# A two-layer encoder kernel: TensorE's work is issued by finer due times, head turns one transposition at a time, and a layer's first weight tiles are split in another order

## The chip, the cores and the metric

One core of a Trainium2 chip. The metric is the device time of the kernel in microseconds. Engines: PE is TensorE's matmul, PEld its weight load, DVE is VectorE, ACT is ScalarE, SP starts the DMA transfers of the weights, POOL is nearly unused.

## The reference, cut to what matters

```python
DEPTH = 2; SEQ = 512; D_MODEL = 1024
def hybrid_layer(x, ...):
    h = rms_norm(x, norm1_g)
    (a_q, a_k, a_v, b_q, b_k, b_v, c_qkv, d_cq, d_ckv, d_kr, gates) = split(h @ w_in)
    oa = windowed_gqa(a_q, a_k, a_v, ...)            # A: 8 heads, window 128
    ob = differential_attention(b_q, b_k, b_v, ...)  # B: 4 heads x 2 maps, all keys, then rms_norm
    oc = dilated_attention(c_qkv, ...)               # C: three patterns C0, C1, C2
    od = latent_attention(d_cq, d_ckv, d_kr, ...)    # D: q and k from low ranks, 8 heads
    merged = sum(sigmoid(gates_i) * (o_i @ w_branch[i]) for the four)
    x = x + merged @ w_o
    u = depthwise_conv(rms_norm(x, norm2_g) @ ffn_w_up)
    g, up = split(u)
    return x + (silu(g) * up) @ ffn_w_down
```

## The kernel before

Both layers are one loop body. Each engine has its own program, written by several streams (Python generators) that are merged: a stream yields a due time, and `together` always lets the stream with the smallest due time emit its next piece. The due times are in steps of TensorE's dense work; `ORDER` gives each block of dense matmuls its START and END. The merged order is fixed when the program is built; on the chip the engines meet through semaphores only.

Dense work (`dense`, `block`): a block is one projection of 512 columns for the 512 tokens, in four PSUM banks (PJ). A weight tile of two 128-row chunks is used by all four banks, one bank a step. The weights arrive in float32; ScalarE rounds a tile to a high half `wh` (L776), VectorE takes the rest as `wl` (L1139), and each product is three float32r matmuls, high by high, high by low, low by high (`split3`, L452 to L454). With two chunks that is six matmuls a step, 24 for a tile, 96 for a block of 16 steps. Tiles are held in three slots, raw tiles in two; SP sends for raw tile k when tile k-2 has been split (`tile_split`). In the blocks of C1 and C2 the tokens are taken in the order of their residues modulo 4, so TensorE's stationary operand is read with a stride of four elements (`perm` in `tokens_out`).

Turns (`turns`, `turn`): once a block of queries or keys is evacuated and normed by VectorE, each 128-token tile is turned by up to four transpositions (L503) into the bank TD, from where ScalarE and VectorE each copy half. `turn` waits for the norm (`normed`) and for TD's last copies, then issues its transpositions. There are 69 turns in a layer. The due times of a block's four turns are 2 steps apart (1.25 or 1.5 for some).

Attention (`attention`): a unit is one head of one query tile. TensorE makes its scores S (L655) into S1, VectorE adds the bias and takes the minimum, ScalarE takes the exponential (L1019), TensorE transposes the probabilities T (L503) into TA, ScalarE copies one half (L1027) and VectorE, behind it, the other (L1563), TensorE multiplies by the values V (L665) into O1. `WINDOW` gives each pattern a stretch of steps, which `slots` divides evenly: with the pace p of a unit, S is due at the start, V of the unit two earlier a third of p later, T of the unit one earlier two thirds later. C0 runs beside the blocks of C1, C1 and C2 beside those of C2, kv and cq, D mostly in a pause without dense work, A beside Bq, Bk and Bv, B beside gate3a to br3b (gates and branch projection of D's output).

The dense stream yields once a step, so S, V, T and turns are only placed between whole steps. A float32 matmul shows two records, a transposition one.

After pattern B, `turns` of VectorE norms oB, and four turns bring it to gTh/gTl for br1a. ScalarE issues the parameter transfers for the next layer behind the last gate of gate3a (L874).

A layer begins with the squares of x on ScalarE (L833), the norm's scale on VectorE (L1208 to L1214), the splits of the first three weight tiles, the copy of the turned parameters (`params_in`, L1063, L1065, L1646), and then eight chunks of transpositions of the normed x (L539), each copied by ScalarE (L841) and VectorE (L1221). The transpositions wait for the parameters' copy, since TD is one of their banks.

## Time and profile before

| | us |
|---|---|
| median of 3 runs | 3001.43 (2998.47 to 3010.02) |
| the profiled execution | 3004.72 |
| its span | 3002.9 |
| TensorE busy in it | 2820.7 (94%), 13358 matmuls |
| TensorE weight loads | 2267.0 (75%) |
| VectorE busy | 1566.0 (52%) |
| ScalarE busy | 1179.0 (39%) |
| DMA moved | 217.62 MB, mean 72 GB/s |

The busy time of TensorE is from the start of a matmul to its modelled end, and neighbours overlap: a dense matmul is listed with 0.39 us, while the next starts 0.23 us later. Distances between starts are what can be added up. A row of a timeline with x4 holds four like instructions in a row. Stretches of the table by windows are the blocks of the first layer, found by counting dense matmuls (96 to a block): 112.9 to 246.6 is C1q, C1k, C1v; 655.7 to 700.4 is Bq; 846.2 to 884.2 is br3a; 957.8 begins gate0a; 1152 to 1495 is most of the feed-forward part.

### The profile page before, as it was taken

What the parts mean: (1) busy time and instruction counts of PE and PEld (TensorE: products, weight loads), DVE (VectorE), ACT (ScalarE), POOL (GpSimd) and SP (SyncE); (2) the same over time, 40 slices, a digit from 0 to 9 for tenths busy, and PEclk for the clock granted to TensorE, in tenths of its full rate; (3) what the DMA queues carried; (4) which work ended last, traced back from release to release, by engine and by line L of the source; (5) the groups of instructions that cost most, each with busy time, mean ns of one, the idle gap of its engine ahead of it and who ended that gap; (6) DMA issues with size and microseconds to landing.
All of it is one profiled execution on the core that took longest, in us unless ns stands there. A gap on an engine that the chain in (4) does not pass through costs nothing.

```text
span 3002.9 us, 44753 instructions
## 1 busy us (share of the span) xinstructions
PE 2820.7 (94%) x13358; PEld 2267.0 (75%) x13358; DVE 1566.0 (52%) x3238; ACT 1179.0 (39%) x2387; POOL 0.6 (0%) x5
## 2 busy tenths in 40 slices
PE   5999989989989998999979999898899899999998
PEld 4889978666667887888868898776666678788887
DVE  5454476444445445555644544764354454465655
ACT  4444444434433234332434444534444332342432
POOL 0000000000000000000000000000000000000000
PEclk9999999889999999999989999999999999999999
DMA  4212222001112332333332122220111123223332
GB/s 152 72 48 72 78 63 85 12 29 41 45 37 78 94 96 78 99 98 99 99 100 64 44 78 79 67 85 1 36 43 50 31 91 98 92 85 98 95 96 91
DMA packets 141819, 217.62 MB, mean 72 GB/s; under 512 B 14777, under 2 KB 69387, under 8 KB 141195
## 3 DMA queue, kind: packets, MB, share of 16 engines
q1 hardware_dynamic: 132521, 200.62, 21.4%
q10 hardware_dynamic: 9058, 14.06, 1.4%
q8 instruction: 118, 1.93, 0.3%
q14 instruction: 122, 1.00, 0.1%
HBM read 206.20 MB, written 8.45 MB: 71 GB/s over the span
## 4 chain that ended last, share of the span: by engine, by line
PE 81%; DVE 9%; ACT 4%; issue 4%; ACTq 1%; DMA 1%; DVEq 0%; SPq 0%
PE bank L452 21%; PE bank L454 20%; PE bank L453 20%; PE bank L665 7%; PE bank L655 6%; PE bank L503 5%; DVE s_work L1563 1%; DVE s_wl L1139 1%; ACT s_wh L776 1%; ACT s_work L1027 1%; DVE s_work L1294 1%; PE bank L539 1%; ACTq L874 1%; DMA s_raw<-in_w_in 0%; ACT s_work L1019 0%
## 5 line engine op out<-in xcount | busy, mean ns | idle before, releaser
L1139 DVE TENSOR_TENSOR s_wl<-s_raw,s_wh 128x1024 fp32r<-128x1024 f32 (+2 forms) x372 | 453.6, 1220 | 526.5 <-ACT s_wh L776 525.9
L776 ACT ACTIVATE s_wh<-s_raw 128x1024 fp32r<-128x1024 f32 (+2 forms) x372 | 392.2, 1055 | 625.1 <-PE bank L454 591.9
L452 PE MATMUL bank<-s_hTh,s_wh 128*128 128x512 f32 x1216 | 486.2, 400 | 4.5 <-DVE s_work L1231 4.5
L454 PE MATMUL bank<-s_hTh,s_wl 128*128 128x512 f32 x1216 | 476.9, 392 | 0.0
L453 PE MATMUL bank<-s_hTl,s_wh 128*128 128x512 f32 x1216 | 476.7, 392 | 0.0
L452 PE MATMUL bank<-s_wh,s_hTh 128*128 128x512 f32 (+1 forms) x1088 | 475.8, 437 | 0.0
L454 PE MATMUL bank<-s_wh,s_hTl 128*128 128x512 f32 (+1 forms) x1088 | 427.0, 392 | 0.0
L453 PE MATMUL bank<-s_wl,s_hTh 128*128 128x512 f32 (+1 forms) x1088 | 426.7, 392 | 0.0
L1019 ACT ACTIVATE s_work<-s_work,s_stat 128x128 f32<-128x128 f32 (+3 forms) x384 | 214.1, 558 | 369.5 <-DVE s_stat L1588 123.0
L1563 DVE COPY s_work<-bank 128x256 f32<-128x256 f32 (+1 forms) x288 | 105.2, 365 | 394.5 <-ACT s_work L1027 391.9
L503 PE MATMUL bank<-s_consts,s_work 128*128 128x128 f32 (+1 forms) x1560 | 250.0, 281 | 47.3 <-DVE s_gTl L1495 14.3
L452 PEld LDWEIGHTS bank<-s_wh,s_hTh 128*128 128x128 f32 x1088 | 252.5, 232 | 47.9 <-issue 24.3
L452 PEld LDWEIGHTS bank<-s_hTh,s_wh 128*128 128x128 f32 x1216 | 230.1, 189 | 67.2 <-issue 16.7
L454 PEld LDWEIGHTS bank<-s_wh,s_hTl 128*128 128x128 f32 x1088 | 252.6, 232 | 27.2
L453 PEld LDWEIGHTS bank<-s_wl,s_hTh 128*128 128x128 f32 x1088 | 256.5, 236 | 20.9 <-issue 0.5
L655 PE MATMUL bank<-s_work 64*128 64x384 f32 (+4 forms) x640 | 267.6, 511 | 1.4 <-DVE s_work L1584 0.9
L454 PEld LDWEIGHTS bank<-s_hTh,s_wl 128*128 128x128 f32 x1216 | 230.1, 189 | 49.3
L453 PEld LDWEIGHTS bank<-s_hTl,s_wh 128*128 128x128 f32 x1216 | 230.3, 189 | 44.5
L503 PEld LDWEIGHTS bank<-s_consts,s_work 128*128 128x128 f32 (+1 forms) x1560 | 193.3, 148 | 89.1 <-DVE s_gTl L1495 17.0
L665 PEld LDWEIGHTS bank<-s_work 128*128 128x128 f32 x1280 | 167.4, 193 | 100.8 <-DVE s_work L1563 48.8
L665 PE MATMUL bank<-s_work 128*128 128x64 f32 (+1 forms) x1280 | 183.1, 280 | 31.4 <-DVE s_work L1563 30.6
L1027 ACT ACTIVATE s_work<-bank 128x256 f32<-128x256 f32 (+1 forms) x288 | 102.8, 357 | 201.0 <-PE bank L503 181.0
(166 smaller groups left out, 3199.6 us busy)
## 6 DMA issues: line engine op xcount, KB each, us to landing
s_raw<-in_w_in SPq DMA_DIRECT2D x168, 512.0 KB, 3.4
s_raw<-in_ffn_w_up SPq DMA_DIRECT2D x176, 256.0 KB, 2.9
s_raw<-in_ffn_w_down SPq DMA_DIRECT2D x44, 512.0 KB, 3.7
s_raw<-in_w_branch SPq DMA_DIRECT2D x32, 512.0 KB, 3.6
s_raw<-in_w_o SPq DMA_DIRECT2D x16, 512.0 KB, 3.6
x_keep<-s_work ACTq DMA_DIRECT2D x2, 2048.0 KB, 7.5
s_raw<-in_w_in SPq DMA_DIRECT2D x16, 256.0 KB, 2.9
s_work<-x_keep ACTq DMA_DIRECT2D x2, 2048.0 KB, 8.2
```

The source lines that it names most:

```text
L452: mm(out, stationary[0], moving[0], start=start, stop=False)
L453: mm(out, stationary[0], moving[1], start=False, stop=False)
L454: return mm(out, stationary[1], moving[0], start=False, stop=stop)
L503: last = nc.tensor.transpose(dst[0:m, n * P:n * P + k], src, ident[0:k, 0:k])
L539: last = nc.tensor.transpose(dst[:, t * P:t * P + P], h_sb[:, t, P * c:P * c + P], ident)
L655: last = mm(out, st, mv, start=True, stop=True)
L665: last = mm(out, st, mv, start=start, stop=stop)
L776: a(wh[:, k % 3, 0:n], raw[:, s, 0:n], ACT.Copy).then_inc(*hi_split.up(own))
L1019: a(probs[:, u % 2, x0:x0 + w], scores[:, u % 2, x0:x0 + w], ACT.Exp, scale=-1.0, bias=stat[:, mins, c:c + 1], accum_out=stat[:, sums, c:c ...
L1027: a(probsT[:, u % 2, P * lo:P * mid], src[:, P * lo:P * mid], ACT.Copy).then_inc(*ta_act.up(own))
L1139: v.tensor_tensor(wl[:, k % 3, 0:n], raw[:, k % 2, 0:n], wh[:, k % 3, 0:n].bitcast(F32), ALU.subtract).then_inc(*tile_split.up(own))
L1563: v.tensor_copy(probsT[:, u % 2, P * mid:P * hi], src[:, P * mid:P * hi]).then_inc(*ta_dve.up(own))
```

## The change

Four things, of which the first three move TensorE's instructions and none changes what is computed. (1) `block` yields before every dense matmul, at sixths of a step, so all other pieces are placed between single matmuls. (2) A turn's transpositions are yielded a sixth of a step apart, so that dense matmuls stand between them; its semaphore is raised by the last. Transpositions of attention keep together (pace 0). (3) Pattern B's window ends at START["gate1a"] - 4 instead of START["gate0a"], 91 steps long instead of 47; `B_NORM` is that end, and the norm of oB, its turns (B_NORM + 9 on) and their copies follow it, as does the transfer that brings x back. (4) At the start of a layer, ScalarE splits tiles 0 and 1 before the squares and tile 2 behind the second chunk of the norm; VectorE splits tile 0 before the norm, tile 1 behind the copy of the parameters, tile 2 behind the second chunk.

```diff
@@ -141,8 +141,9 @@
     END[name] = START[name] + steps
 WINDOW = dict(
     C0=(START["C1q"] + 1, START["C2q"], 32), C1=(START["C2q"] + 1, START["kv"], 8), C2=(START["kv"] + 1, START["gate2a"], 8),
-    D=(START["Aq"] + 14, START["Bq"], 32), A=(START["Bq"], START["gate3a"], 32), B=(START["gate3a"] + 1, START["gate0a"], 32),
+    D=(START["Aq"] + 14, START["Bq"], 32), A=(START["Bq"], START["gate3a"], 32), B=(START["gate3a"] + 1, START["gate1a"] - 4, 32),
 )
+B_NORM = WINDOW["B"][1]
 def build(nc, io):
@@ -447,11 +448,9 @@
             holder = [(pj_dve, b - 3) for b in range(4)]
-            def split3(out, stationary, moving, start, stop):
-
-                mm(out, stationary[0], moving[0], start=start, stop=False)
-                mm(out, stationary[0], moving[1], start=False, stop=False)
-                return mm(out, stationary[1], moving[0], start=False, stop=stop)
+            def split3(stationary, moving):
+
+                return (stationary[0], moving[0]), (stationary[0], moving[1]), (stationary[1], moving[0])
             def block(name, ntiles, operands, by, chunks=2, cols=512, width=512, first=lambda i, b: None):
@@ -468,9 +467,13 @@
                             taken[by] += 1
                             holder[b] = (by, taken[by])
                         first(i, b)
+                        n = 0
                         for c in range(chunks):
-                            st, mv = operands(b, chunks * i + c, [t[:, c, :] for t in w])
-                            last = split3(PJ[b][:, 0:width], st, mv, i == 0 and c == 0, i == ntiles - 1 and c == chunks - 1)
+                            for st, mv in split3(*operands(b, chunks * i + c, [t[:, c, :] for t in w])):
+                                if n:
+                                    yield START[name] + 4 * i + b + n / (3 * chunks)
+                                n += 1
+                                last = mm(PJ[b][:, 0:width], st, mv, start=i == 0 and n == 1, stop=i == ntiles - 1 and n == 3 * chunks)
                         if i == ntiles - 1:
                             last.then_inc(*pj_ready.up())
                         elif b == 3:
@@ -496,12 +499,14 @@
             H, G = (hTh, hTl), (gTh, gTl)
-            def transposed(dst, sources, at=0):
-
-                for n, src in enumerate(sources, at):
+            def transposed(dst, sources, done, when, pace, at=0):
+
+                for n, src in enumerate(sources):
+                    if n:
+                        yield when + n * pace
                     k, m = src.shape[0], src.shape[1]
-                    last = nc.tensor.transpose(dst[0:m, n * P:n * P + k], src, ident[0:k, 0:k])
-                return last
+                    last = nc.tensor.transpose(dst[0:m, (at + n) * P:(at + n) * P + k], src, ident[0:k, 0:k])
+                last.then_inc(*done.up())
             def turned(n):
@@ -585,14 +590,15 @@
                             *hidden_lo.at(l, hidden + 2 * i + 2)) if half == "a" and b == 0 else None)
                     hidden += 2 * size
-            def turn(sources, *ready):
-
+            def turn(when, sources, *ready):
+
+                yield when
                 for handle, count in ready:
                     pe.wait_ge(handle, count)
                 pe.wait_ge(*td_act.at(l, n_turn[0]))
                 pe.wait_ge(*td_dve.at(l, n_turn[0]))
-                transposed(TD, sources).then_inc(*td_ready.up())
                 n_turn[0] += 1
+                yield from transposed(TD, sources, td_ready, when, 1 / 6)
             def turns():
@@ -601,9 +607,8 @@
                 def head_turns(begin, sources_of, pace=2.0):
                     nonlocal n
                     for t in range(4):
-                        yield begin + pace * t
                         n += 1
-                        turn(sources_of(t), normed.at(l, n))
+                        yield from turn(begin + pace * t, sources_of(t), normed.at(l, n))
                 def chunks_of(src):
                     return lambda t: [src[:, t, P * c:P * c + P] for c in range(4)]
...
@@ -627,8 +631,7 @@
                 yield from head_turns(END["Bq"] + 6, chunks_of(stage))
                 yield from head_turns(END["Bk"] + 6, chunks_of(stage))
                 for t in range(4):
-                    yield START["gate0a"] + 10 + 1.25 * t
-                    turn([oB[:, t, P * c:P * c + P] for c in range(4)], sublayer_normed.at(l, t + 1))
+                    yield from turn(B_NORM + 9 + 1.25 * t, [oB[:, t, P * c:P * c + P] for c in range(4)], sublayer_normed.at(l, t + 1))
             def attention(name, scores_of, values_of, per_out, begun, keys=all_keys, tile_of=None):
@@ -644,7 +647,7 @@
                         pe.wait_ge(*ta_act.at(l, n_att[0]))
                         pe.wait_ge(*ta_dve.at(l, n_att[0]))
                         n_att[0] += 1
-                        transposed(TA, tile_of(tile)).then_inc(*ta_ready.up())
+                        yield from transposed(TA, tile_of(tile), ta_ready, at, 0)
                     if step < n:
                         yield at
                         if step == 0:
@@ -673,7 +676,7 @@
                         pe.wait_ge(*ta_dve.at(l, n_att[0]))
                         n_att[0] += 1
                         group[u] = n_att[0]
-                        transposed(TA, [probs[:, u % 2, P * k:P * k + P] for k in range(lo, hi)], at=lo).then_inc(*ta_ready.up())
+                        yield from transposed(TA, [probs[:, u % 2, P * k:P * k + P] for k in range(lo, hi)], ta_ready, at + 2 * pace / 3, 0, at=lo)
             def token_values(v_of, width, places, keys=all_keys):
                 def values_of(u, out, pt):
...
@@ -832,9 +835,11 @@
                         act.wait_ge(*own.done(l))
                         a(h_sb[:, t, cols], x_sb[:, t, cols], ACT.Square, accum_out=stat[:, 0, 4 * half + t:4 * half + t + 1]).then_inc(*ssum.up(own))
-            def norm_out(row):
+            def norm_out(row, after_two=lambda: None):
                 for c in range(DC):
+                    if c == 2:
+                        after_two()
                     n_norm[0] += 1
                     act.wait_ge(*nt_ready.at(l, n_norm[0]))
                     act.wait_ge(*own.done(l))
...
@@ -1055,15 +1060,15 @@
                 act.wait_ge(*x_moved.at(l, 1))
                 act.dma_start(x_sb, keep).then_inc(*x_moved.up())
+            split_next()
+            split_next()
             squares(-8)
-            for _k in range(3):
-                split_next()
             src = group()
             act.wait_ge(*own.done(l))
             a(prm[:, 0:NROW], src[:, 0:NROW], ACT.Copy).then_inc(*act_step.up(own))
             act.wait_ge(*own.done(l))
             a(prm[:, NROW:NROW + 88], src[:, P:P + 88], ACT.Copy).then_inc(*td_act.up(own))
-            norm_out(ROW["norm1"])
+            norm_out(ROW["norm1"], split_next)
             act.dma_start(keep, x_sb).then_inc(*x_moved.up())
             for n, name in enumerate(("d_q_norm", "d_k_norm")):
                 direct(rope_rows[:, n, :], io[name][L, NOPE:DQK].broadcast_to([P, ROPE]))
...
@@ -1509,7 +1516,7 @@
                 yield from q_out(END["Aq"] + 6, qA, 0)
                 yield from q_out(END["Bq"] + 6, qT, 4)
                 yield from k_out(END["Bk"] + 6, kT, "bk")
-                begin = START["gate0a"] + 1
+                begin = B_NORM
                 for t in range(4):
                     yield begin + 2 + 0.9 * t
                     dve.wait_ge(*own.done(l))
@@ -1636,20 +1643,20 @@
                                      keys=near_keys, tile_at=4)
                 yield from attention("B", biased_b, out_b, 4)
+            split_next()
             normalise()
-            for _k in range(3):
-                split_next()
             dve.wait_ge(*params_in.at(l, 0))
             src = group()
             dve.wait_ge(*own.done(l))
             v.tensor_copy(prm[:, NROW + 88:NROW + 176], src[:, 256:344]).then_inc(*td_dve.up(own))
+            split_next()
             for at, n, key in ((0, 4, "aq"), (4, 4, "bq"), (8, 12, "cqn")):
                 dve.wait_ge(*own.done(l))
                 v.tensor_scalar(gain[:, at:at + n], consts[:, 128 + at:128 + at + n], prm[:, ROW[key]:ROW[key] + 1], None, ALU.mult).then_inc(*dve_step.up(own))
             dve.wait_ge(*own.done(l))
             v.tensor_scalar(gain[:, 21:22], prm[:, ROW["dq"]:ROW["dq"] + 1], -DQK ** -0.5, None, ALU.mult).then_inc(*gains_in.up(own))
-            norm_out(ROW["norm1"])
+            norm_out(ROW["norm1"], split_next)
             together(dense(), turns(), attentions(), splits())
     for name, s in signals.items():
```

## Rows read from the trace of the kernel before

**Rows 1.** The page: the span, and the chain that ended last, by engine.

```profile
span 3002.9 us, 44753 instructions
...
PE 81%; DVE 9%; ACT 4%; issue 4%; ACTq 1%; DMA 1%; DVEq 0%; SPq 0%
```

**Rows 2.** Busy time by stretches: length, each engine's busy us, granted clock, DMA share, GB/s.

```profile
112.90:246.60 133.70, 132.49 (x626) 109.91 (x626) 60.26 (x164) 56.21 (x140) 0.00 (x0) 1.00 0.16 49
...
655.70:700.40 44.70, 42.29 (x194) 29.38 (x193) 17.34 (x46) 18.86 (x55) 0.00 (x0) 0.97 0.20 60
...
846.20:884.20 38.00, 30.54 (x135) 21.02 (x133) 13.24 (x31) 9.70 (x21) 0.00 (x0) 0.87 0.10 31
...
1152.00:1495.00 343.00, 343.00 (x1516) 284.08 (x1517) 203.75 (x240) 128.46 (x154) 0.00 (x0) 1.00 0.31 96
```

**Rows 3.** Timeline of TensorE in C0v: start us, listed us, engine, line, operation.

```profile
98.73 0.60 PE L503 MATMUL bank<-s_consts,s_work 128*128 128x128 f32 x4
...
99.40 0.40 PE L453 MATMUL bank<-s_wl,s_hTh 128*128 128x512 f32 x1
```

**Rows 4.** The same in C2k, where tokens are read with a stride.

```profile
303.11 0.39 PE L454 MATMUL bank<-s_wh,s_hTl 128*128 128x512 f32 x1
303.34 0.60 PE L503 MATMUL bank<-s_consts,s_work 128*128 128x128 f32 x4
...
304.13 0.40 PE L453 MATMUL bank<-s_wl,s_hTh 128*128 128x512 f32 x1
```

**Rows 5.** The same in C1q, strided too: scores (L655) and values (L665).

```profile
145.40 0.91 PE L655 MATMUL bank<-s_work 64*128 64x384 f32 x2
...
146.70 0.40 PE L453 MATMUL bank<-s_wl,s_hTh 128*128 128x512 f32 x1
...
150.22 0.91 PE L655 MATMUL bank<-s_work 64*128 64x384 f32 x2
151.06 0.88 PE L665 MATMUL bank<-s_work 128*128 128x64 f32 x6
151.78 0.50 PE L503 MATMUL bank<-s_consts,s_work 128*128 128x128 f32 x3
...
154.58 0.88 PE L665 MATMUL bank<-s_work 128*128 128x64 f32 x6
...
155.71 0.40 PE L453 MATMUL bank<-s_wl,s_hTh 128*128 128x512 f32 x1
```

**Rows 6.** The same in gate3a, where nothing is strided.

```profile
821.53 1.12 PE L655 MATMUL bank<-s_work 64*128 64x512 f32 x2
...
822.92 0.39 PE L453 MATMUL bank<-s_hTl,s_wh 128*128 128x512 f32 x1
...
826.90 1.12 PE L655 MATMUL bank<-s_work 64*128 64x512 f32 x2
827.95 1.16 PE L665 MATMUL bank<-s_work 128*128 128x128 f32 x8
```

**Rows 7.** Timeline at the start of the second layer, VectorE and TensorE.

```profile
1515.09 0.16 DVE L1208 TENSOR_TENSOR s_stat<-s_stat 128x4 f32<-128x4 f32 x1 [2.64 <-issue]
...
1520.54 2.35 DVE L1139 TENSOR_TENSOR s_wl<-s_raw,s_wh 128x1024 fp32r<-128x1024 f32 x2
...
1528.13 0.25 DVE L1646 COPY s_prm<-bank 128x88 f32<-128x88 f32 x1
...
1534.29 0.47 PE L452 MATMUL bank<-s_wh,s_hTh 128*128 128x512 f32 x1
```

**Rows 8.** Timeline of TensorE in br3a; in brackets the idle time before.

```profile
858.42 2.08 PE L665 MATMUL bank<-s_work 128*128 128x128 f32 x8 [7.46 <-DVE s_work L1563]
```

**Rows 9.** Timeline of VectorE and TensorE at the start of gate0a.

```profile
956.89 0.68 DVE L1231 SCALAR_TENSOR_TENSOR s_work<-s_work,bank 128x512 f32<-128x512 f32 x1
...
973.05 1.42 DVE L1524 TENSOR_TENSOR s_work<-s_work,s_stat 128x512 f32<-128x512 f32 x2
...
973.96 0.65 PE L503 MATMUL bank<-s_consts,s_work 128*128 128x128 f32 x4 [1.05 <-DVE s_work L1524]
```

More of the change, by code:

```diff
@@ L616, in turns @@
                 for t in range(4):
-                    yield END["cq"] + 14 + 1.5 * t
-                    turn([oC[:, 0, t, P * c:P * c + P] for c in range(4)], combined.at(l, t + 1))
+                    yield from turn(END["cq"] + 14 + 1.5 * t, [oC[:, 0, t, P * c:P * c + P] for c in range(4)], combined.at(l, t + 1))
                 for hb in range(2):
                     for t in range(4):
-                        yield END["dq1"] + 13.2 + 5 * hb + 1.25 * t
-                        turn([(stage, stage_b)[hb][:, t, DQK * h:DQK * h + DQK] for h in range(4)], normed.at(l, n + 1))
+                        yield from turn(END["dq1"] + 13.2 + 5 * hb + 1.25 * t,
+                                        [(stage, stage_b)[hb][:, t, DQK * h:DQK * h + DQK] for h in range(4)], normed.at(l, n + 1))
                 n += 1
@@ L730, in _ @@
             pe.wait_ge(*params_in.at(l, 0))
-            turn([rows[:, n, :] for n in range(3)])
+            together(turn(0, [rows[:, n, :] for n in range(3)]))
             together(dense(), turns(), attentions())
@@ L989, in turns @@
                 for t in range(4):
-                    yield START["gate0a"] + 10.4 + 1.25 * t
+                    yield B_NORM + 9.4 + 1.25 * t
                     hi_out(gTh[:, 0:4, P * t:P * t + P], group(), td_act, gain[:, 20:21])
@@ L1214, in normalise, with norm_out @@
                     v.tensor_scalar(h_sb[:, t, :], x_sb[:, t, :], stat[:, 2, t:t + 1], None, ALU.mult).then_inc(*h_normed.up(own))
-            def norm_out(row):
+            def norm_out(row, after_two=lambda: None):
                 for c in range(DC):
+                    if c == 2:
+                        after_two()
                     n_norm[0] += 1
```

## The prediction

> **What bounds the kernel now.** I read the page first: the profiled execution took 3004.72 us around a span of 3002.9 us, and 81% of the chain that ended last lies on TensorE's matmuls [rows 1]. Then a table by stretches. In the feed-forward part (1152 to 1495) TensorE is busy all the time, 1516 matmuls in 343.00 us, 0.226 us each; the change touches nothing there. In the stretch of the second dilated pattern's projections (112.9 to 246.6) it is busy 132.49 of 133.70 us, so whatever is added to its queue lengthens the kernel. From 655.7 it idles a few per cent, and from 846.2 to 884.2 it idles 7.5 us at a granted clock of 0.87 [rows 2]. So for most of what the diff touches the question is what TensorE's own queue costs in its new order, and only in a few places which wait goes. Then the timeline, for the price of one neighbour beside another, since a matmul's listed duration overlaps the next and only distances between starts add up.
>
> **The order.** TensorE's order follows from the due times alone (`together` takes the smallest), so it can be written out for both kernels. A step is one bank's six dense matmuls, 6 x 0.227 = 1.36 us. Before, everything else lands only between whole steps, and parts due within one step form one run ("V6 T3"). After, each dense matmul has a due time of its own, so scores S, values V and transpositions T, due a third of a unit apart, land apart. Counting in both orders how often a run ends and a dense matmul follows (an "exit"), per layer: T 112 before, 342 after; V 56 and 112; S 58 and 114. Of these, in the six blocks C1q to C2v, whose stationary operand is read with a stride of four ("strided"): T 28 and 92, V 23 and 40, S 23 and 40. The numbers of matmuls stay the same.
>
> **Price of an exit.** Plain: four T start at 98.73 and the second dense matmul behind them at 99.40. Taking off one dense distance, 0.227, and three T-to-T distances of 0.109 (the start listed for the first dense one is modelled early, so I go by the second), the last T to the first dense one takes 0.116 [rows 3]. That is 0.007 more than T to T: a plain exit is nearly free. Strided: 303.34 to 304.13, less 0.235 (the distance of dense neighbours there, 0.23 at 303.11) and 0.327, leaves 0.228 [rows 4]: 0.119 more than T to T, because the strided weights are loaded behind only a short transposition. V: six V and then T take 151.06 to 151.78, 0.72; six V and then the dense one take 154.58 to 155.71 less 0.235, 0.895: an exit costs 0.175. S: two S and then V take 0.84, two S and then the dense one 146.70 - 145.40 - 0.235 = 1.065: 0.225 [rows 5]. Plain S: 822.92 - 821.53 - 0.227 = 1.16 against 827.95 - 826.90 = 1.05: 0.11 [rows 6]. Plain V lies at 0.175 less the 0.112 by which strided and plain differ for T: 0.06; I take that for the 64-column V of pattern A and nothing for the 128-column ones. Going from a dense matmul into T or V costs nothing beyond the dense distance (0.23 at 303.11) [rows 4], and into S as much as before.
>
> The sum per layer: strided 64 x 0.119 + 17 x 0.175 + 17 x 0.225 = 7.6 + 3.0 + 3.8 = 14.4 us. Plain: T 166 x 0.007 = 1.2, V 22 x 0.06 = 1.3, S 39 x 0.11 = 4.3, together 6.8. So 21 us a layer, 42 in both. Of it the split of the turns themselves is small: 69 turns x 3 new exits, 48 of them strided (the four turns each of C1q, C1k, C2q and C2k, which fall beside strided blocks): 48 x 0.119 + 159 x 0.007 = 6.8 us a layer, 14 in both; the rest is the finer grid. The row that is missing is a T alone between two dense matmuls. From below: if the next dense weights were fetched together with the T's under one long matmul, the exit would cost nothing and the T less than its 0.109; from above: nothing suggests over 0.228 for strided ones. I take the measured exits, since the loads in every row run one ahead.
>
> The Trainium skill ("TensorE: Matmul & The Clock Gate", LDWEIGHTS) says that a load takes its number of columns over 1.2 GHz, 107 ns, whatever else. The plain rows agree (0.109 and 0.116), the strided ones do not (0.228); by the rule the strided exits would cost as the plain ones and the sum would be some 14 us smaller for T alone. The same page (Step-by-step) lets the engine pull loads ahead of matmuls in flight through a deep window; what that would make of this change is the second rival.
>
> **Start of a layer.** Before, in the second layer: the sum of squares is ready and VectorE starts at 1515.09, normalises until 1520.6, splits tiles 0 and 1, waits for tile 2 (whose transfer waits for tile 0's split), splits it, and only then copies the parameters at 1528.13, for which the norm's transpositions wait; the first dense matmul starts at 1534.29, 6.2 us later [rows 7]. After: VectorE splits tile 0 first (1.22 us), normalises (5.5), and copies at about 1522.0. ScalarE's two splits now stand before its squares, which costs it nothing before the last squares' data arrive except some 1 us of queue, hidden by VectorE's first split. Behind the copy VectorE has one split (1.22) more before the norm's low halves and one more after two chunks; the last transpositions wait for VectorE's chunks, so from copy to the first dense matmul I count 7 instead of 6.2. First dense at about 1529: 5 us earlier. In layer 0 the two splits of ScalarE delay the squares by 2.8 instead; gain 3. Together -8 (0 if the copy is no longer last, -13 if nothing is added behind it). Moving tile 0's split forward also lets SP's transfer of tile 2 start some 5 us sooner, off the path.
>
> **Pattern B's window** runs over 91 instead of 47 steps. Its work is the same, with more cover: before, 5 of 32 units have no dense matmul between a unit's T and V; after, at least 10. But its two large waits stay. In br3a TensorE waits 7.46 us [rows 8] while ScalarE issues 15 parameter DMAs in a row, behind which the copy of a transposed tile is queued; at half the density TensorE has some 3 us more of other work: -3 (0 to -10, with the low clock behind it). At the end, oB is normed on VectorE beside the branch's own evacuation: before, that took from 956.89 to 973.05 and the first turn waited 1.05 us [rows 9]. That turn was due 10 steps behind the block that it follows; now it is due 5 behind br0b. Same work (16 us), 5 steps (6.8 us) less cover, dense tile splits between: the first oB turn waits about 6, and with its transpositions spread over half a step the three next ones about 1 each, +5 against before (0 to +9). Small waits -2. Net 0 a layer (-12 to +9).
>
> **Pattern A's window**: T to V is 6 dense matmuls before in all 32 units and 5 after; the waits there (some 10 us a layer) stay. A third or so of the plain 6.8 us falls where TensorE waits anyway: -1.5 a layer. Turns on VectorE's heels (cq, oC) are paced by VectorE and keep their time. Splitting any turn delays its completion by three dense matmuls, 0.7 us; at a pace of 2 steps (2.7 us) that is covered.
>
> **Sum.** +42 - 3 - 8 + 0 = +31 us on the profiled execution. The median shown (3001.43) lies 3.3 below that execution; the difference is applied to the median: 3032 us.
>
> **Rivals.**
> (1) The forecast: exits as priced, waits about as before. 3015 to 3050, likeliest 3032. Chance 0.65.
> (2) Faster: the loads hide. If one 512-column matmul covers both the T's load and that of the dense one behind it, exits cost nothing, and each spread T costs about half its present 0.109, so a turn (0.44 us now) saves 0.22. Decides from the point at which two loads fit ahead. 138 turns x 0.22 = 30, plus 8 from the start: 2963; if only the exits are free, 2993. Against it: in the rows a dense load behind a T is never cheaper than T to T. Chance 0.12, at about 2978.
> (3) No difference: the finer places take the waits for ScalarE's and VectorE's copies out of patterns A and B. Up to 20 us a layer are there (7.46 of it the DMA burst); all gone, 42 - 40 - 8 = -6: 2995. Against it: T to V grows only in B, and the two large waits have other causes. Chance 0.15, at about 3003.
> (4) Slower still: the copies come too late in C0 as well, since T to V is 5 dense matmuls instead of 6 in 26 of its 32 units; 0.3 us x 32 x 2 = +19, and the waits at oB drop the clock: 3055. Chance 0.08.
> That the change does only what its title says is no case: the diff puts every part on the finer grid. If it did (turns alone), the sum would be 14 - 8 = +6.
>
> About 0.5%, 15 us, can be told from no change. Slower by more (over 3016): 0.73; within: 0.16; faster: 0.11. The range from 2993 to 3054 leaves out most of (2) and the tail of (4).
>
> **What would show it.** Exits: C1q to C1v longer by about 11 us a layer (133.7 to 145) at full clock with no new idle time, C2q to C2v by 3; T alone between dense matmuls at 0.23 behind the one before, and 0.34 (plain) or 0.46 (strided) from T to the second dense one. Start: the copy of the parameters within 7.5 us of the sum of squares and the first dense matmul 5 us sooner. B: a wait of 4 to 5 us in br3a and one of about 6 before the oB turns in gate1a. It would be wrong if spread T in strided blocks showed T to dense well below 0.2, or if pattern A lost its waits.

## The result, and the profile after

The changed kernel takes 3025.99 us (median; 3021.69 to 3030.5), 1.0073 of the time before (95% interval 1.0054 to 1.0092): slower, by 24.6 us at the medians, each of five executions. The profiled execution of after took 3021.69 us around a span of 3019.9, that of before 3004.72: 17.0 us between the two that are compared below. The page of after, against [rows 1]: the same number of instructions, a longer span, and one point more of the chain on TensorE.

```profile
span 3019.9 us, 44753 instructions
...
PE 82%; DVE 8%; issue 4%; ACT 3%; ACTq 1%; DMA 0%; DVEq 0%; SPq 0%
```

The table by stretches, with the columns of [rows 2]: the dilated pattern's strided blocks C1q to C1v, Bq, br3a, gate1a, the feed-forward part.

```profile
110.50:252.60 142.10, 142.01 (x626) 114.39 (x626) 60.59 (x164) 56.68 (x140) 0.00 (x0) 1.00 0.15 47
664.60:708.90 44.30, 44.02 (x195) 29.92 (x194) 17.39 (x46) 19.32 (x56) 0.00 (x0) 0.93 0.20 60
837.00:863.70 26.70, 22.63 (x94) 15.60 (x93) 9.59 (x18) 6.08 (x12) 0.00 (x0) 0.87 0.15 44
1023.70:1057.10 33.40, 26.46 (x114) 19.76 (x113) 20.39 (x36) 8.68 (x11) 0.00 (x0) 0.95 0.21 64
1157.00:1500.00 343.00, 342.94 (x1516) 284.06 (x1515) 203.98 (x241) 128.59 (x155) 0.00 (x0) 1.00 0.31 96
```

C1q to C1v were 133.7 us and are 142.1, with the same 626 matmuls, TensorE busy throughout and the clock at full: the loss is in the queue's own order. The feed-forward part is unchanged. br3a has lost 11 of its 38 us, since its window ends later, and still idles 4 us. gate1a idles 6.9, where it had no idle time before (21.8 us long then).

Cut by the first dense matmul of each block, with starts from the timeline, both layers together (the 8.3 us behind the last dense matmul are in neither column):

| us | before | after | difference |
|---|---|---|---|
| to the first dense matmul | 43.2 | 39.5 | -3.7 |
| C0q to C0v | 139.5 | 141.9 | +2.4 |
| C1q to C2v (strided) | 458.8 | 482.0 | +23.2 |
| kv to gate2b, dk (turns of cq, dq) | 356.8 | 366.0 | +9.2 |
| Aq and the pause behind it | 262.5 | 260.3 | -2.2 |
| Bq to Bv (pattern A) | 281.7 | 273.9 | -7.8 |
| gates and branches (pattern B) | 597.0 | 598.0 | +1.0 |
| o0, o1 | 114.3 | 114.1 | -0.2 |
| feed-forward, without its last block | 685.7 | 685.7 | 0 |
| down2b, start of layer 1 in it | 55.2 | 50.2 | -5.0 |

The row of Aq hides two things. From the first to the last of Aq's own 96 dense matmuls a layer it is +5.2 us (52.7 to 57.9, all at full clock), and the pause behind them is -7.4 (209.8 to 202.4), with 28.9 us at the low clock instead of 41.7.

### The profile page after: what moved, and what is told of

The parts are those of the page before. It is cut to its first block, busy times and chain, and to the rows that moved or that the text cites. A ratio compares the mean times of both kernels' runs of the same rounds, so it can differ in the third digit from the quotient of the medians.

```text
span 3019.9 us, 44753 instructions
## 1 busy us (share of the span) xinstructions
PE 2855.5 (95%) x13358; PEld 2258.9 (75%) x13358; DVE 1567.3 (52%) x3238; ACT 1179.7 (39%) x2387; POOL 0.6 (0%) x5
## 4 chain that ended last, share of the span: by engine, by line
PE 82%; DVE 8%; issue 4%; ACT 3%; ACTq 1%; DMA 0%; DVEq 0%; SPq 0%
PE bank L476 63%; PE bank L668 7%; PE bank L658 7%; PE bank L508 6%; DVE s_wl L1144 1%; DVE s_work L1570 1%; ACT s_work L1032 1%; ACT s_wh L779 1%; DVE s_work L1301 1%; ACTq L879 1%; PE bank L544 0%; DMA s_raw<-in_w_in 0%; DVE s_work L1304 0%; DVE s_gTl L1471 0%; ACT s_work L1024 0%
## 5 line engine op out<-in xcount | busy, mean ns | idle before, releaser
L476 PE MATMUL bank<-s_hTl,s_wh 128*128 128x512 f32 x1216 | 487.9, 401 | 0.0
L476 PE MATMUL bank<-s_hTh,s_wl 128*128 128x512 f32 x1216 | 487.1, 401 | 0.0
L476 PE MATMUL bank<-s_wl,s_hTh 128*128 128x512 f32 (+1 forms) x1088 | 474.6, 436 | 0.0
L476 PE MATMUL bank<-s_wh,s_hTh 128*128 128x512 f32 (+1 forms) x1088 | 461.2, 424 | 0.0
L476 PE MATMUL bank<-s_wh,s_hTl 128*128 128x512 f32 (+1 forms) x1088 | 460.3, 423 | 0.0
L508 PE MATMUL bank<-s_consts,s_work 128*128 128x128 f32 (+1 forms) x1560 | 311.0, 280 | 55.4 <-DVE s_gTl L1502 13.4
L508 PEld LDWEIGHTS bank<-s_consts,s_work 128*128 128x128 f32 (+1 forms) x1560 | 203.2, 143 | 112.2 <-issue 19.5
L476 PEld LDWEIGHTS bank<-s_wh,s_hTh 128*128 128x128 f32 x1088 | 254.5, 234 | 43.6 <-issue 18.9
L668 PEld LDWEIGHTS bank<-s_work 128*128 128x128 f32 x1280 | 174.0, 193 | 33.0 <-DVE s_work L1570 15.2
L668 PE MATMUL bank<-s_work 128*128 128x64 f32 (+1 forms) x1280 | 172.0, 272 | 13.4 <-DVE s_work L1570 13.0
```

What stands on the lines that cost most here:

```text
L476: last = mm(PJ[b][:, 0:width], st, mv, start=i == 0 and n == 1, stop=i == ntiles - 1 and n == 3 * chunks)
L508: last = nc.tensor.transpose(dst[0:m, (at + n) * P:(at + n) * P + k], src, ident[0:k, 0:k])
L668: last = mm(out, st, mv, start=start, stop=stop)
```

## Experiments

"By trace" is the difference of such cuts against the kernel before, or against the kernel named, both layers together. The number behind a median is its ratio to the kernel before on the same chip, with its 95% interval. Of each edit the main lines are shown.

### One part at a time

**e1_start**: the kernel before with the new order at a layer's start.

```
-            squares(-8)
-            for _k in range(3):
-                split_next()
+            split_next()
+            split_next()
+            squares(-8)
```

> The kernel before with part (4) of the change alone: tiles 0 and 1 split by ScalarE before the squares, tile 0 by VectorE before the norm, tile 1 behind the parameters' copy, tile 2 behind the second chunk. Theory: the first dense matmul of a layer comes 3.6 us sooner in layer 0 and 5.1 in layer 1 (as in the changed kernel's trace), nothing else moves: -8 to -9 us, about 2993. Rival: part of it is given back at the next wait: under -4.

Measured 2996.22 us, 0.9972 (0.9955 to 0.9988). By trace the first dense matmul comes 4.1 us sooner in layer 0, and the last block with layer 1's start is 5.1 shorter: 9.2, as forecast.

**e4_bwin**: the kernel before with pattern B's longer window alone.

```
-B=(START["gate3a"] + 1, START["gate0a"], 32)
+B=(START["gate3a"] + 1, START["gate1a"] - 4, 32)
```

> The kernel before with pattern B's window of 91 steps alone, on whole steps, turns together, old start. Theory: the wait at the DMA burst shrinks from 7.5 to about 4 us and its low clock with it, a wait of 5 to 6 us before the oB turns comes in gate1a: -2 to -5 us a layer, about 2994. Rival (B's stalls are in its own units and go with the cover): -10 a layer, about 2981; or the oB wait eats all: same.

Measured 2999.32 us, 0.9982 (0.9969 to 0.9994): a gain of some 5 us by the ratio, by trace 4.3 in gates and branches. br3a idles 4.0 instead of 7.5 a layer, gate1a 4.9 and 5.3 instead of 0. The window trades one wait for another and keeps a little.

**e2_grid**: the change without split turns, without the new start and window: dense matmuls and attention on the fine grid.

```
-                yield from transposed(TD, sources, td_ready, when, 1 / 6)
+                yield from transposed(TD, sources, td_ready, when, 0)
```

> Due times at sixths of a step for the dense work, but each turn's transpositions together, pattern B's old window and the old start. Theory of exits: C1q to C2v +10 us a layer (26 T, 17 V and 17 S exits in strided blocks), in plain blocks +6 of exits, of which pattern A gives back more by shorter waits: +14 to +22 in all, about 3018. Rival (the finer grid is for free, the turns cost): within 4 us of before.

Measured 3007.35 us, 1.0009 (0.9996 to 1.0022): far less than expected. By trace +2.3, of very unequal parts: strided blocks +13.0, C0 +2.2, kv to dk +1.1, gates -1.8, pattern A -6.9 (idle 17.8 to 8.3), and -6.2 in Aq and its pause, nearly all of it the clock (below). The strided exits are there. Pattern A's waits are mostly gone, against the prediction; the expectation of this run had allowed for that, but not for so little from the plain exits.

**e3_turns**: the opposite half: split turns, attention back on whole steps, old start and window.

```
-                        yield at
+                        yield math.floor(at) + 0.99
```

> A turn's transpositions one at a time between dense matmuls, all of attention kept between whole steps, old window, old start: what the title says. Theory of exits: 48 exits in strided blocks at 0.12 us are +5.7 us a layer in C1k, C1v, C2k, C2v, and up to 3 a layer of waits for later turns in C0k, dq0 and gate2b: +11 to +18 in all, about 3015. Rival (loads hide behind the dense matmul): -10 or faster.

Measured 3045.15 us, 1.0135 (1.0116 to 1.0155), twice the upper end expected. By trace +36.9: strided blocks 13.9, kv to dk 9.1, gates 5.1, C0 2.4, pattern A 1.6, Aq 2.6. Two of these are no exits at all: 9.1 where the turns follow VectorE closely, and the 5.1.

**e9_together**: the changed kernel with a turn's transpositions together again, all else kept (the edit of e2_grid on it).

> The changed kernel with each turn's transpositions together again (pace 0), all else as changed. Theory after e1 to e4: start -8, grid +3 and window -5 leave -10 against the kernel before, so the turns' split alone is worth 30 us or more of the changed kernel: about 2996 (before 3006). Of it 10 in the strided blocks, 8 in the stretch kv to br2b, 4 in the gates. Rival (the split's cost in e3 came from its attention on whole steps): 3012 to 3018.

Measured 3010.1 us, 1.0021 (1.0004 to 1.0037), against 1.0073: splitting the turns costs 0.5%, some 16 us by the medians, 19 between the lowest executions. By trace the changed kernel is longer by 10.1 in the strided blocks, 8.1 in kv to dk, 2.7 in the gates and 3.5 in Aq's own matmuls, together 24. Against it stand the pause behind Aq and pattern A (-3.7), where this execution had more low clock (47.9 us instead of 28.9, and 20.3 instead of 11.9). Which of 16 and 24 is nearer stays open. The prediction had 14, the expectation of this run 30, too much weight on e3_turns.

### Is it the stride?

**e5_plain_b** and **e6_plain_a**: before and after, with the tokens of C1 and C2 read in their stored order. The two patterns then work on the wrong tokens; instructions and shapes are the same.

```
-tokens_out(H, perm=j > 0)
+tokens_out(H)
```

> The kernel before with the tokens of C1 and C2 read in their own order, not strided (so these two patterns work on the wrong tokens; the work is the same). It is the partner of e6_plain_a. Theory: the 28 T, 23 V and 23 S exits of these blocks each cost 0.11 us less, and 576 dense matmuls a layer take 0.227 instead of 0.235: 2 x (8.1 + 4.6) = -25 us, about 2976.

> The changed kernel with the same alteration (tokens of C1 and C2 unstrided, so computed on the wrong tokens). Theory: 92 T, 40 V and 40 S exits each 0.11 us cheaper and the dense matmuls as in e5_plain_b: 2 x (18.9 + 4.6) = -47 us against the changed kernel, so that the two unstrided kernels lie within 5 us of each other. Rival (the cost of the change is not in the strided exits): they differ as before and after do, by 20 to 25 us.

Measured 2981.17 us, 0.9918 (0.9892 to 0.9943), and 2984.41, 0.9922 (0.9899 to 0.9946). Strided, the two kernels lie 0.73% apart, unstrided 0.04% by these ratios (intervals of 0.25% either way) and 3.2 us by the medians. The table by stretches of C1q to C1v, e5_plain_b and then e6_plain_a:

```profile
112.90:240.30 127.40, 126.05 (x626) 91.54 (x625) 60.08 (x164) 55.91 (x140) 0.00 (x0) 1.00 0.18 51
```

```profile
110.70:237.90 127.20, 126.97 (x625) 89.10 (x624) 59.79 (x164) 56.18 (x140) 0.00 (x0) 1.00 0.18 51
```

Without the stride the same order is 0.2 us shorter instead of 8.4 longer. Over all six blocks the difference is +1.0 (436.1 to 437.1), with 1.3 less idle time in it, instead of +23.2, with 2.0 less: so 22.2 of the 23.2 is the stride (22.9 with the idle time taken out of both), and a plain exit costs almost nothing.

### What the finer grid gives back, and why turns wait

**e12_short**: the changed kernel with turns split only at a pace of two steps; those at 1.25 and 1.5 (dq, dk, oB, oC) go together.

```
-yield from transposed(TD, sources, td_ready, when, 1 / 6)
+yield from transposed(TD, sources, td_ready, when, spread)   # 1/6 where pace == 2.0, else 0
```

> The changed kernel with only those turns together whose due times are less than 2 steps apart (oC, dq, dk, oB); the other turns stay split. Theory: a split turn ends 0.7 us later, and where turns follow each other every 1.25 or 1.5 steps the next one waits for the bank's copies: gate2b goes back from 29.5 to about 27.5 and dq0 from 9.6 to 8.5 a layer, gate1a loses 1.5: -8 to -11 us against the changed kernel. Rival (the spread costs by its exits everywhere alike): -1.

Measured 3020.11 us, 1.0051 (1.0027 to 1.0074). By trace dq0, gate2b and gate1a are 1.2, 1.8 and 1.6 us a layer shorter than after, 9.2 in both, and Aq's own matmuls another 1.75 a layer. The medians lie 5.9 us apart, with overlapping intervals. The profiled execution is longer than after's all the same, by 13.3: Aq and its pause alone make +19.9, with 92.5 us at the low clock instead of 28.9.

Two turns of after that follow VectorE, all engines (TensorE's loads are PEld; those of dense matmuls left out):

```profile
492.55 0.31 PE L508 MATMUL bank<-s_consts,s_work 128*96 128x128 f32 x1 [0.38 <-DVE s_work L1269]
...
493.62 0.27 PE L508 MATMUL bank<-s_consts,s_work 128*96 128x128 f32 x1
...
493.93 0.47 ACT L930 ACTIVATE s_work<-bank,s_gain 96x256 f32<-96x256 f32 x1 [2.46 <-PE bank L508]
...
494.43 0.48 DVE L1463 TENSOR_SCALAR s_work<-bank,s_gain 96x256 f32<-96x256 f32 x1 [0.97 <-ACT s_work L930]
...
494.96 0.12 PEld L508 LDWEIGHTS bank<-s_consts,s_work 128*96 128x96 f32 x1 [0.58 <-DVE s_work L1463]
494.97 0.32 PE L508 MATMUL bank<-s_consts,s_work 128*96 128x128 f32 x1
```

And turns of e12_short at the same place, TensorE:

```profile
491.19 0.64 PE L508 MATMUL bank<-s_consts,s_work 128*96 128x128 f32 x4 [0.21 <-DVE s_work L1269]
493.29 0.60 PE L508 MATMUL bank<-s_consts,s_work 128*96 128x128 f32 x4
495.59 0.60 PE L508 MATMUL bank<-s_consts,s_work 128*96 128x128 f32 x4
```

The bank that a turn writes is free again only when ScalarE and VectorE have copied it, one behind the other. Split, a turn's last transposition starts 1.07 behind its first, the copies take until 494.91, and the loads of the next turn wait 0.58 for that (releaser DVE L1463): the turns start 2.42 apart, where together they start 2.10 and 2.30 apart. A pace of 1.25 steps is 1.70 us of dense matmuls and 0.44 of the turn, 2.14: it had no room for the 0.7 us more.

### The two waits that stayed

**e8_burst**: the changed kernel with the 15 parameter DMAs issued in another place.

```
-if i == 3 and half == "a":
+if i == 1 and half == "b":
```

> The changed kernel with ScalarE's parameter transfers behind gate1b instead of gate3a, where no attention runs. Theory: the wait of 4.1 us in br3a and its low clock vanish, and nothing waits behind the burst in its new place: -6 to -8 us a layer, -12 to -16 against the changed kernel. Rival (it collides there with the tile splits or merged sums, whose readers have less cover): -5 or less.

Measured 3034.37 us, 1.0097 (1.0066 to 1.0127): no faster than the change itself (1.0073), though the wait aimed at is gone. The table by stretches of e8_burst, br3a and br1b up to o0's first matmul:

```profile
838.20:858.30 20.10, 20.10 (x93) 13.74 (x92) 9.71 (x18) 6.20 (x12) 0.00 (x0) 1.00 0.19 53
1084.10:1102.00 17.90, 11.03 (x49) 8.83 (x48) 5.83 (x8) 5.12 (x7) 0.00 (x0) 0.94 0.12 40
```

br3a is free of idle time (4.1 in the changed kernel) and the stretch of br1b, which had none, has 6.9, all of it before o0's first matmul. There the burst held back ScalarE's split of a weight tile by 9.95 us, and VectorE, which waits for that split, was late with the evacuation of the branch. The wait went where the burst went: the burst is its cause. ScalarE in the kernel before shows its length: the first and the last of the 15 issues, and the copy behind them.

```profile
847.50 0.87 ACTq L874 DMA_DIRECT2D s_rows<-in_norm_g  x2
...
856.92 0.30 ACTq L874 DMA_DIRECT2D s_rows<-in_ffn_conv_b  x1
857.43 0.39 ACT L1027 ACTIVATE s_work<-bank 128x256 f32<-128x256 f32 x1 [9.56 <-issue]
```

**e7_ob_late**: the changed kernel with oB's turns due 5 steps later on TensorE.

```
-yield from turn(B_NORM + 9 + 1.25 * t,
+yield from turn(B_NORM + 14 + 1.25 * t,
```

> The changed kernel with TensorE's four oB turns due 5 steps later (B_NORM + 14). Theory: the wait of some 7 us before them in gate1a and its low clock vanish, since VectorE's norm is then done: -6 to -9 us a layer, -12 to -18 against the changed kernel. Rival (the wait moves to br1a, which needs what they turn): the same as the changed kernel.

Measured 3021.75 us, 1.0038 (1.0018 to 1.0057). Against the changed kernel it is 4 us by the medians and 10 by the ratios, and by trace gate1a is 4.3 us a layer shorter (idle 6.9 to 4.0). The expectation was 12 to 18 us; the copies on ScalarE and VectorE had kept their old places in those engines' queues, which I take for the rest without having run it alone. If so, an order written for three engines has to be moved on all three.

**e10_roomy** puts the lessons together on the kernel before: new start, whole steps, turns together; pattern B's window ends 12 steps before the changed kernel's, oB's turns stand 4 steps further behind its end, on all three engines, and the parameter DMAs go out one in ten steps.

```
+B=(START["gate3a"] + 1, START["gate1a"] - 16, 32)
+for n, (dst, src) in enumerate(parameter_rows((DEPTH - 1) - l)):
+    yield START["up0"] + 6 + 10 * n
+    act.dma_start(...)
```

> The kernel before with the new start, pattern B's window ending at START[gate1a] - 16 (79 steps), the oB turns 13 steps behind it on all three engines, and ScalarE's parameter transfers one by one, ten steps apart, in the feed-forward part. Whole steps, turns together. Theory: -8 by the start, the DMA wait and its low clock (12 us a layer before) and the oB waits (5 a layer) gone: 8 + 2 x 15 = -38 us, less some for what is late next: 2966 to 2980. Rival (another wait takes their place in the gates): -15 or less.

Measured 2972.36 us, 0.9886 (0.9859 to 0.9913). By trace gates and branches are 569.2 instead of 597.0, with 2.7 us of idle time instead of 24.1; the parts of this edit were not run one by one. The table for br3a and gate1a of e10_roomy:

```profile
825.40:846.90 21.50, 21.25 (x104) 14.80 (x101) 11.35 (x25) 6.88 (x14) 0.00 (x0) 1.00 0.19 50
1005.70:1028.60 22.90, 22.53 (x103) 18.39 (x102) 8.37 (x10) 7.30 (x9) 0.00 (x0) 1.00 0.30 89
```

**e11_fineA** adds the fine grid in the three blocks where e2_grid gained.

```
+if n and name in ("Bq", "Bk", "Bv"):
+    yield START[name] + 4 * i + b + n / (3 * chunks)
```

> e10_roomy with due times at sixths of a step in Bq, Bk and Bv only, none of which is strided. Theory: pattern A's waits shrink as in e2_grid (idle 17.8 to 8.3 us in both layers, -7 in time), nothing is paid elsewhere: 6 to 8 us below e10_roomy. Rival (the waits went in e2_grid because what came before was slower): the same as e10_roomy.

Measured 2963.44 us, 0.9865 (0.9842 to 0.9888), the fastest kernel here. Pattern A idles 7.5 us instead of 16.8, both layers. Its blocks are not shorter by trace (280.7 against 279.7), though 9.3 us of idle time are gone: 28.3 us of them ran at the low clock in this execution, 11.7 in that of e10_roomy; how much of the 9 us between the medians is the edit and how much the clock stays open, and the two intervals overlap.

## Why the prediction was right, and where it was not

Direction, order of size and the named mechanism (strided exits) held: the median came out 6 us under the forecast and within the range. On the profiled executions, where the sum was made, it was 17.0 against 31. That gap has causes, given below, and they show that so near a hit was in part luck.

**Exits in strided blocks: right.** Counted in the traces, the exits are as forecast (92 T, 40 V and 40 S a layer in these blocks). Forecast +11 for C1q to C1v and +3 for C2q to C2v a layer, without idle time; measured +8.4 and +3.1. Their price above plain ones was forecast at 14.4 - 3.3 = 11.1 a layer (3.3 is the same 64 T, 17 V and 17 S at the plain prices), 22.2 in both; e5_plain_b and e6_plain_a give 23.2 - 1.0 = 22.2 (that it fits to the tenth is chance; without idle time it is 22.9). The distances are the ones named. TensorE's timeline of after, strided (C1k) and plain:

```profile
176.43 0.27 PE L508 MATMUL bank<-s_consts,s_work 128*128 128x128 f32 x1
176.46 0.60 PE L476 MATMUL bank<-s_wh,s_hTh 128*128 128x512 f32 x1
176.90 0.27 PE L508 MATMUL bank<-s_consts,s_work 128*128 128x128 f32 x1
```

```profile
492.94 0.27 PE L508 MATMUL bank<-s_consts,s_work 128*96 128x128 f32 x1
492.96 0.48 PE L476 MATMUL bank<-s_hTh,s_wh 128*128 128x512 f32 x1
493.28 0.27 PE L508 MATMUL bank<-s_consts,s_work 128*96 128x128 f32 x1
```

0.47 strided and 0.34 plain from one T to the next, with one dense matmul between. It is so throughout: over the 92 such distances of the strided blocks, both layers, the median is 0.465, and in e6_plain_a, in the same blocks without the stride, 0.343. Rival 2 (half of 0.109 for the T, 0.227 for the dense one) would have had 0.28, so the load behind the T does not hide. The Trainium skill ("TensorE: Matmul & The Clock Gate", Step-by-step) lets loads be pulled ahead of matmuls in flight. For the load behind a T these distances show no gain from that.

**Plain exits: mis-sized.** The term of 6.8 a layer rested on the plain S (0.11) and V (0.06) [rows 6], taken from one pair of distances each or from a difference. In C1 and C2 without the stride these prices make 6.7 in both layers; the runs give 1.0, or 2.3 with the idle time that went. The other plain blocks, as far as they have no new wait, show nothing either (C0 +2.4, of which 2 x 1.1 is a wait). I should have taken the plain S and V with the bound of zero for the sum and not for the range alone.

**Pattern A's waits: wrong.** "T to V is 6 dense matmuls before in all 32 units and 5 after; the waits there (some 10 us a layer) stay" counted matmuls on TensorE and not what stands ahead of the copy on ScalarE. Who waited for VectorE's copy of a transposed tile, us and times, before:

```profile
  PEld bank L665: 9.6, 10
  PE bank L665: 5.3, 9
```

and after:

```profile
  PEld bank L668: 2.7, 4
  PE bank L668: 2.4, 4
```

The timeline of before, TensorE and ScalarE:

```profile
689.85 0.50 PE L503 MATMUL bank<-s_consts,s_work 128*128 128x128 f32 x3
...
690.57 0.60 ACT L1019 ACTIVATE s_work<-s_work,s_stat 128x384 f32<-128x384 f32 x1
...
691.17 1.04 ACT L776 ACTIVATE s_wh<-s_raw 128x1024 fp32r<-128x1024 f32 x1
...
692.12 0.36 ACT L1027 ACTIVATE s_work<-bank 128x256 f32<-128x256 f32 x1
...
693.03 0.88 PE L665 MATMUL bank<-s_work 128*128 128x64 f32 x6 [0.46 <-DVE s_work L1563]
```

and of after:

```profile
688.33 0.49 ACT L1024 ACTIVATE s_work<-s_work,s_stat 128x256 f32<-128x256 f32 x1
...
688.82 1.04 ACT L779 ACTIVATE s_wh<-s_raw 128x1024 fp32r<-128x1024 f32 x1
688.95 0.38 PE L508 MATMUL bank<-s_consts,s_work 128*128 128x128 f32 x2
...
689.77 0.25 ACT L1032 ACTIVATE s_work<-bank 128x128 f32<-128x128 f32 x1
...
691.15 0.55 PE L668 MATMUL bank<-s_work 128*128 128x64 f32 x4
```

On whole steps scores, values and transpositions go in one run, so the exponential of the new scores (and here a split) stands on ScalarE between the transpositions and their copy: 2.3 us from one to the other. In the unit of after the exponential is done before them: 0.8 us. These are two clear units. Over all 64 copies of ScalarE in pattern A the mean distance from the last transposition fell from 1.09 to 0.69 us, and those over 1.2 us from 25 to 12. The idle time fell from 17.8 to 7.8 us with everything, to 8.3 with the grid alone, and from 16.8 to 7.5 in e11_fineA: three pairs agree on what the grid does, while the reason is read from the timelines. The prediction had named the loss of these waits as a sign of being wrong. Rival 3 was right about this one place and wrong about the rest.

**Turns close behind VectorE: wrong.** "Turns on VectorE's heels (cq, oC) are paced by VectorE and keep their time" did not hold for oC, and "at a pace of 2 steps (2.7 us) that is covered" left out those at 1.25 and 1.5. The 0.7 us of delay was counted, the chain behind it (two copies, then the bank is free) was not. Price: gate2b +2.6 and dq0 +1.3 us a layer. e12_short and e9_together take back 1.8 and 1.2 of it; the last 0.8 of gate2b is there with the turns together too (e2_grid), so it belongs to the grid. The eight turns of dk, due beside Aq's matmuls, pay as well. Who waits there on TensorE's loads in after: us, times, longest.

```profile
PEld bank L508 <- DVE s_work L1463: 3.4, 7, 0.6
```

In e9_together it is 0.6 us, twice. Aq's 96 matmuls take 26.4 us a layer in every kernel whose turns go together and whose attention is on whole steps there, 27.2 on the fine grid with these turns together (e2_grid, e9_together, e12_short) and 29.0 in after: 1.75 a layer for the split. So the split of the turns cost 16 us by the medians and 24 by trace, not 14, and of a different make: 10.1 of strided exits (11.4 forecast) and the rest waits.

**The tie, not seen.** C0k has a new wait, on TensorE:

```profile
74.55 0.33 PE L508 MATMUL bank<-s_consts,s_work 128*128 128x128 f32 x1 [1.37 <-DVE s_work L1466]
```

It stands with the turns together too (e2_grid), so it isn't the split. An item due at a whole step was taken behind that step's six dense matmuls; now only the first of the six is due as early, and the item goes ahead of the other five, 1.1 us sooner. For C0k's turn that is before its source is ready. The shift is not what made gate1a slower than in e4_bwin (31.5 us long): with the turns together it is 31.8 (e9_together, e12_short), split 33.4. There too it is the split.

**Start: right.** VectorE's timeline in after, at layer 1, against [rows 7]:

```profile
1520.33 1.22 DVE L1144 TENSOR_TENSOR s_wl<-s_raw,s_wh 128x1024 fp32r<-128x1024 f32 x1 [2.52 <-issue]
1521.59 0.16 DVE L1213 TENSOR_TENSOR s_stat<-s_stat 128x4 f32<-128x4 f32 x1
...
1527.14 0.25 DVE L1652 COPY s_prm<-bank 128x88 f32<-128x88 f32 x1
```

From VectorE's last instruction of layer 0 (1520.33 less 2.52 idle) to the copy it is 9.3 us; before it was 15.7 (1528.13, less 1515.09 and 2.64). From the copy to the first dense matmul (1534.57) it is 7.4 us, before 6.2, forecast 7. So 5.1 gained here for the 5 forecast, 3.7 in layer 0 for 3; e1_start alone gains 9.2 in both.

**Pattern B's window: right in kind.** Forecast a wait of 4 to 5 us in br3a and about 6 before oB's turns, net 0. TensorE in after:

```profile
850.15 1.23 PE L668 MATMUL bank<-s_work 128*128 128x128 f32 x4 [4.07 <-DVE s_work L1570]
```

```profile
1029.70 0.50 PE L476 MATMUL bank<-s_hTh,s_wh 128*128 128x512 f32 x1 [1.11 <-DVE s_work L1238]
1036.41 0.47 PE L508 MATMUL bank<-s_consts,s_work 128*128 128x128 f32 x1 [3.47 <-DVE s_work L1531]
1040.56 0.33 PE L508 MATMUL bank<-s_consts,s_work 128*128 128x128 f32 x1 [0.56 <-DVE s_gTl L1471]
1043.67 0.33 PE L508 MATMUL bank<-s_consts,s_work 128*128 128x128 f32 x1 [0.61 <-DVE s_gTl L1471]
```

4.07 for the first; for the second, where some 6 and then 1 at each later turn were forecast, 3.47 at the turns, 1.11 ahead of them at the branch's evacuation and about 0.6 at two later turns. Net +1.0 in both layers.

**The balance** on the profiled executions, from the 31.4 of the sum to 17. Strided blocks 23.2 for 28.8: -5.6. Plain exits -11.2: 13.6 was taken, and 2.4 is all that the other blocks grew by once the terms named here are out. Pattern A -7.8 for -3: -4.8. The start -0.7. The 2.4 is a remainder and was measured nowhere by itself. Not in the sum at all: gate2b and dq0 +7.8, the split turns beside Aq +3.5, C0's tie +2.2, and what is left of Aq and its pause, mostly the clock (below), -5.7. Together -14.5. Without that last term the two executions would lie some 23 us apart, an estimate, near the 24.6 of the medians. So the forecast of 31 was some 8 us too high, and it came that near because 22 us too much in its terms and 13.5 us of waits that it had not seen cancel in part.

## What to carry to other kernels

Before work is put on a finer grid between matmuls, price the load behind each short neighbour by its operand's stride: here only strided operands made it dear, and there short matmuls in a group were cheaper. A finer order also moves what the other engines find in their queues: follow each item to its copy and to the bank it frees, and check what falls at a tie of due times. Moving a burst of DMA issues moves its wait with it; spreading it, and giving the norm ahead of oB's turns its own time, together took 28 us out of the gates and branches (597.0 to 569.2). Before two profiles are compared, set aside the stretches whose clock differs, but look in them for a part at full clock: Aq's +5.2 stood there.

## What the hardware showed that was not expected

**A strided load.** In [rows 4] the load behind a short transposition takes 0.228 us where the plain one takes 0.116 [rows 3], and after has 0.47 against 0.34 from turn to turn. The Trainium skill ("TensorE: Matmul & The Clock Gate", LDWEIGHTS) gives a load's time by its columns alone, over 1.2 GHz, which makes an estimate of 107 ns for the 128 here. The plain rows agree, the strided ones do not, and taking the stride out removed 22.2 of 23.2 us. Dense matmuls hide most of it: removing the stride from the kernel before made the six blocks 22.7 us shorter over both layers (458.8 to 436.1).

**The clock in one stretch.** The pause behind Aq has no stable length, though Aq and the pause have the same instructions in all kernels. The table by stretches for one kernel, e9_together, its layers 0 and 1, and then e12_short's layer 0:

```profile
524.76:661.35 136.59, 120.77 (x610) 86.92 (x608) 62.08 (x158) 53.02 (x127) 0.00 (x0) 0.87 0.06 16
2015.95:2144.93 128.98, 111.87 (x609) 79.35 (x608) 61.75 (x158) 52.91 (x127) 0.00 (x0) 0.95 0.06 17
```

```profile
531.28:671.83 140.55, 126.33 (x609) 91.35 (x608) 62.47 (x158) 53.29 (x127) 0.00 (x0) 0.84 0.05 16
```

VectorE and ScalarE do the same work in the same time; TensorE's busy time and the length go with the granted clock. Over the executions profiled, the time at 1.2 GHz instead of 2.4 in this stretch is 19.5 to 92.5 us for both layers, and its length 254.5 to 280.2. The same kernel, e9_together, has 7.6 us between its two layers. So two profiled executions can differ by some 20 us with no cause in the order, and differences here were taken block by block. Before and after have nearly the same time at the low clock in pattern A (12.8 and 11.9 us) and in the gates and branches (20.5 and 20.4), but not in kv to dk (17.0 and 23.9), where I took no account of it.
